# Whole sets of early weight forms, activation tiles in freed form slots, and a last quarter ended in halves: three edits to a decoder-layer kernel on eight cores

## What is computed

```python
u = rms_norm(h, norm_mix_pre)
proj = u @ w_in                      # q, k, v of two attention branches, forget logits, two gates
o_sb, o_fx = stick_breaking(...), forgetting_softmax(...)
merged = sigmoid(g_sb) * (o_sb @ w_branch_sb) + sigmoid(g_fx) * (o_fx @ w_branch_fox)
h = h + rms_norm(merged @ w_out, norm_mix_post)
u2 = rms_norm(h, norm_ffn_pre)
ff = (silu(u2 @ w_gate) * (u2 @ w_up)) @ w_down      # d_ff 5632
return h + rms_norm(ff, norm_ffn_post)
```

## Time and profile before

| what | value |
|---|---|
| median of 3 runs | 3856.3 us (lowest 3856.13) |
| the profiled execution's own time | 3855.46 us |
| its span on the slowest core (core 3), first to last instruction | 3853.9 us |
| spans of the 8 cores | 3804.6 to 3853.9 us |
| PE busy in that span | 94% |

### The profile page before, as it was taken

How to read it: one execution, slowest core, us unless ns; L and a number is a source line. 1 busy time by engine, 2 the same in 40 slices (tenths; PEclk the granted TensorE clock), 3 DMA queues, 4 the chain that set the end, 5 groups by cost and what they waited for, 6 DMA issues and landing times.

```text
span 3853.9 us, 63553 instructions; the slowest of 8 cores (3804.6 to 3853.9 us)
## 1 busy us (share of the span) xinstructions
PE 3633.4 (94%) x21572; PEld 1835.9 (48%) x21572; DVE 1664.3 (43%) x2198; ACT 1468.1 (38%) x2339; POOL 652.5 (17%) x659
## 2 busy tenths in 40 slices
PE   5999899999989989999999899999999999999994
PEld 2566566666644434444444344444444443444442
DVE  3657677677743330122154577444445530000104
ACT  3567687778841112211144343333333321111110
POOL 0000000000011110144204532222222210001322
PEclk9889999999999999999999999999999998999997
DMA  8336654555669887577478975333336657448995
GB/s 217 58 65 101 94 81 80 93 89 88 118 134 212 207 199 204 146 165 172 85 246 264 271 247 187 132 110 110 109 108 203 216 171 198 103 103 209 201 223 179
DMA packets 381774, 597.03 MB, mean 155 GB/s; under 512 B 187792, under 2 KB 240400, under 8 KB 369424
## 3 DMA queue, kind: packets, MB, share of 16 engines
q1 hardware_dynamic: 324832, 391.58, 36.6%
q0 software_dynamic: 35888, 163.63, 23.3%
q10 hardware_dynamic: 20736, 37.76, 2.8%
HBM read 566.66 MB, written 124.78 MB: 179 GB/s over the span
## 4 chain that ended last, share of the span: by engine, by line
PE 73%; DMA 12%; DVE 7%; ACT 3%; issue 3%; POOL 1%; SPq 0%; DVEq 0%; ACTq 0%; POOLq 0%
PE ps L80 73%; DMA fd<-pf 5%; DVE pf L80 2%; DMA mh<-mixs 2%; DMA WT<-W 1%; DVE form L80 1%; ACT pf L80 1%; DMA Ost<-On 1%; DMA hbx<-hs 1%; DVE uT L80 1%; DMA mixs<-mixst 1%; DVE F L80 1%; DMA hb<-hs 1%; ACT L80 0%; ACT sq L80 0%
## 5 line engine op out<-in xcount | busy, mean ns | idle before, releaser
L80 PE MATMUL ps<-F,form 128*128 128x512 bf16 x3584 | 798.9, 381 | 18.1 <-ACT sg L80 18.1
L80 PE MATMUL ps<-as,wd 128*128 128x512 bf16 x2816 | 625.6, 382 | 14.2 <-DMA as<-ad 14.2
L80 PEld LDWEIGHTS ps<-F,form 128*128 128x128 bf16 x3584 | 351.3, 98 | 446.1 <-issue 28.0
L80 PE MATMUL ps<-uT,wbf 128*128 128x512 bf16 x2048 | 500.8, 390 | 22.0 <-DVE uT L80 16.1
L80 PE MATMUL ps<-uT,wgA 128*128 128x512 bf16 x2048 | 456.7, 381 | 0.0
L80 PEld LDWEIGHTS ps<-as,wd 128*128 128x128 bf16 x2816 | 276.1, 98 | 353.3 <-issue 25.5
L80 POOL TENSOR_TENSOR sn<-sn,sn 128x512 f32<-128x512 f32 x176 | 243.4, 1388 | 844.7 <-ACT sn L80 831.8
L80 DVE TENSOR_TENSOR form<-stage 128x1024 bf16<-128x1024 f32 x220 | 298.9, 1379 | 127.0 <-PE ps L80 95.6
L80 PE MATMUL ps<-F,formd 128*128 128x512 bf16 x1344 | 313.5, 381 | 10.8 <-ACT sn L80 6.0
L80 PEld LDWEIGHTS ps<-uT,wbf 128*128 128x128 bf16 x2048 | 200.4, 100 | 246.6 <-issue 69.6
L80 PEld LDWEIGHTS ps<-uT,wgA 128*128 128x128 bf16 x2048 | 201.3, 98 | 243.8 <-issue 5.6
(11 more groups left out here) (111 smaller groups left out, 3374.4 us busy)
## 6 DMA issues: line engine op xcount, KB each, us to landing
stage<-wgu_s SPq DMA_DIRECT2D x44, 2048.0 KB, 9.6
wd<-wfd_t POOLq DMA_DIRECT2D x32, 1408.0 KB, 13.6
formd<-fd SPq DMA_DIRECT2D x168, 256.0 KB, 7.3
wgA<-wg_t POOLq DMA_DIRECT2D x64, 512.0 KB, 8.9
wbf<-wqkv_t POOLq DMA_DIRECT2D x48, 512.0 KB, 7.6
ps<-wgu_s SPq DMA_DIRECT2D x24, 1024.0 KB, 12.3
ad<-ao SPq DMA_DIRECT2D x176, 128.0 KB, 5.4
as<-ad SPq DMA_DIRECT2D x22, 1024.0 KB, 17.9
```

What stands on the lines that cost most here:

```text
L80: ins = getattr(eng, meth)(**kw)
```

## The change

Three edits.

1. `pre_make(j)` makes a whole set: one load of 2 MB into the single tile `ps` (16 KB per partition), seven operations of 128x1024, each into the next of six tiles `pf`, each with a store of its own (256 KB). The load of the next set is issued after the last store of the set. It runs at every second tick (after the second block of a channel tile), so that the 12 sets go out in 24 of the 32 ticks.
2. The `as` tiles 4 to 10 take the seven slots of `F[1]`, one by one, in the order in which the last set's steps are finished with them, and each load is issued right behind that step. Other tiles move to make room.
3. At the end, the held channel tiles do the third quarter (512 tokens), then the last quarter in two halves of 256 tokens. Each half has its own statistics bank, whose sum is added on DVE to that of the 13 earlier channel tiles, its own factor, and its own 16 final items of 256 columns. The gain moves into ACT's eviction copy, so the item's first DVE operation is a plain product; all sums of the end are on DVE, none on POOL. The block banks of this part go round in five, not six.

```diff
-    ps = [at(WO + 20 * i, f"ps{i}", [128, 4, 512], F32, dma=True) for i in range(2)]
-    pf = at(WO + 28, "pf", [128, 7, 512], BF16, dma=True)
+    ps = at(WO + 20, "ps", [128, 4, 1024], F32, dma=True)
+    pf = [at(WO + 2 * i, f"pf{i}", [128, 1024], BF16, dma=True) for i in range(6)]
...
     def pre_make(j):
...
+        for x, p in enumerate(PORD):
+            a_, b_, op = FORM_A[p]
+            dst = pf[(7 * j + x) % 6]
...
+            kb.dma(SP, dst.ds, fd[j, x], dst.t[:, :], reads=[dst.r], writes=[fd_res[j][x]])
+        pre_load(j + 1)
...
-    fl = Filler([pre_make(j) for j in range(2 * N0)], 29)
+    pre_load(0)
+    fl = Filler([(lambda j: (lambda: pre_make(j // 2) if j % 2 == 1 else None))(j) for j in range(2 * N0)], 2 * N0)
     P5(0, fl)
...
+    F1_ORDER = (5, 2, 1, 3, 4, 6, 7)
+    a_off = [22 + 8 * i for i in range(4)] + [108 + 8 * FORM_B[p] for p in F1_ORDER] + [56 + 8 * i for i in range(6)]
...
+        s_, p = steps[n]
+        if j == 0:
+            al.kill(F[1][0].r)
+        if s_ == len(sets) - 1:
+            al.kill(F[1][1][FORM_B[p]])
+            i = 4 + F1_ORDER.index(p)
+            mk_as(i)
+            load_a(0, i)
...
-    for gi in range(4, 11):
-        load_a(0, gi)
...
+                kb.op(DVE, "tensor_tensor", dict(out=ft, in0=ft, in1=rstd3.t[:, col:col + w], op=ALU.mult),
+                      reads=[rstd3.r], writes=[fr])
+                kb.op(DVE if tail else POOL, "tensor_tensor", dict(out=ft, in0=ft, in1=hh_.t[:, 0:w], op=ALU.add),
+                      reads=[hh_.r], writes=[fr])
...
+    f0, i0 = final_items([(c_, 2, 0, 512) for c_ in range(KC)], True)
+    f0()
+    subs = [(0, 0, 512), (1, 0, 256), (1, 256, 256)]
...
+        if w < 512:
+            b2, r2 = banks[6 - lo // 256]
+            kb.op(DVE, "scalar_tensor_tensor", dict(out=rstd2.t[:, 0:w], in0=b2[:, lo:lo + w], scalar=1.0 / D,
+                                                    in1=rstd2.t[:, 0:w], op0=ALU.mult, op1=ALU.add),
+                  writes=[r2, rstd2.r])
...
+    for si, (tc, lo, w) in enumerate(subs):
         for c in range(hold_c, KC):
-            b_ = bank()
-            down_mm(1, wd[(KC + c) % 3], b_[0], b_[1], tc, ALLG, False)
+            b_ = banks[nb["d"] % 5]
+            nb["d"] += 1
+            down_mm(1, wd[(KC + c) % 3], b_[0], b_[1], tc, ALLG, lo, w)
...
+                rstd_part(6 + subs[si - 1][0], subs[si - 1][1], subs[si - 1][2], (512 * (si - 1), 512)[si - 1 > 0])
+                if si == 1:
+                    work += i0
+                else:
+                    f1, i1 = final_items([(c_, 3, 0, 256) for c_ in range(KC)], True)
+                    work += [f1] + i1
+                    step(1)
+            down_ev(1, c, tc, *b_, lo, w)
+            if si > 0:
+                step(5 if si == 1 else 4)
+    step(99)
```

More of the change, by code:

```diff
@@ L1112, in pre_make @@
     def pre_make(j):
[L1113 to L1129, removed]
@@ L1464, in _emit, with stat_w, down_ev @@
     pend = []
-    def down_ev(hf, c, tc, bt, br_):
+    def stat_w(bi, sf, c, lo, w):
+        sb_t, sb_r = banks[bi]
+        first, last = (hold_c if w < 512 else 0), (hold_c - 1 if bi == 7 and hold_c < KC and w == 512 else KC - 1)
+        kb.op(PE, "matmul", dict(out=sb_t[:, lo:lo + w], lhsT=ones_bf, rhs=sf.t[:, 0:w], start=(c == first),
+                                 stop=(c == last)), reads=[sf.r, cbf.r], writes=[sb_r])
+    def down_ev(hf, c, tc, bt, br_, lo=0, w=512):
         fs, sf = ffst[nb["m"] % 2], sqf[nb["m"] % 2]
@@ new lines, in _emit, with step, rstd_part @@
+    f0()
+    subs = [(0, 0, 512), (1, 0, 256), (1, 256, 256)]
+    work = []
+    def step(k):
+        while k > 0 and work:
+            work.pop(0)()
+            k -= 1
+    def rstd_part(bi, lo, w, col):
+        bt, br = banks[bi]
+        kb.op(DVE, "tensor_scalar", dict(out=rstd2.t[:, 0:w], in0=bt[:, lo:lo + w], scalar1=1.0 / D, scalar2=EPS,
+                                         op0=ALU.mult, op1=ALU.add), writes=[br, rstd2.r])
+        if w < 512:
[3 more added lines that the diff above has]
+                  writes=[r2, rstd2.r])
+        kb.op(ACT, "activation", dict(out=rstd2.t[:, 0:w], in_=rstd2.t[:, 0:w], func=AF.Ln), writes=[rstd2.r])
+        kb.op(ACT, "activation", dict(out=rstd3.t[:, col:col + w], in_=rstd2.t[:, 0:w], func=AF.Exp, scale=-0.5),
+              reads=[rstd2.r], writes=[rstd3.r])
@@ new lines, in _emit @@
+                if si == 1:
+                    work += i0
+                else:
+                    f1, i1 = final_items([(c_, 3, 0, 256) for c_ in range(KC)], True)
[5 more added lines that the diff above has]
+    step(99)
+    while pend:
+        stat_w(*pend.pop(0))
+    rstd_part(7, 256, 256, 768)
+    f1, i1 = final_items([(c_, 3, 256, 256) for c_ in range(KC)], True)
@@ L1556, in _emit @@
+    f1()
+    work += i1
+    step(99)
     finish()
```

146 lines of the change are left out of this document (63 added, 83 removed).

## The result

The changed kernel takes 3832.0 us (median of 5 runs; 3882.9 us for the kernel before, whose 5 runs include the three that gave 3856.3). The ratio of the two is 0.989, 95% interval 0.985 to 0.993: faster, by about 1%, and by less than the 2% of which the prediction spoke. The ratios here leave out runs in which a die showed a lower clock; the medians contain them. The forecast was 3805.5, a ratio of 0.987, with a range of 3789 to 3838. So the time lies in the range, 26.5 us above the forecast. The change is smaller than it looks from there: 50 us less were forecast, and against the 3856.3 us from which the prediction started 24 came. Why, the parts of the sum show.

What follows compares the result with a forecast made beforehand. PE was taken to bound the kernel, with 94% of the span. From the profiled 3855.5 us, less 35.2 (merge stage) and 21.3 (down start), plus 6.5 (end), came 3805.5 us; range 3789 to 3838.

Steps and rivals of the forecast that it cites:

- I take 21.2: Merge stage: DMA time per set and channel tile in us, 0.5 short of PE's pace; gain 35.2 us.
- the play of 9.5 us: Merge stage: a set may start up to 9.5 us late before PE waits for the next block's products.
- the sets fall behind: Merge stage rival: 23.2 us per set, gain 16, kernel 3825; sets behind or loads late together got chance 0.22.
- the full figure: Merge stage: at 358 GB/s a channel tile's 7.1 MB take 19.8 us, sets just keep pace, gain 39.2 us.
- most of them start before the end, so the last lands at about 3167 to 3173: Down start: early loads of `as4` to `as10`, 20 us for 7.3 MB, leave 0.5 us lost; gain 21.3 us.
- +1.4: Start of the end part: first block reuses the preceding block's bank and waits 1.4 us for its two evictions.
- 2 x (0.426 + 0.11) = 1.07: End: us per half item of 256 columns, two DVE operations with gaps; 16 items take 17.1 us.
- the span ends 8.0 us later: End: in the kernel before, the span ends 8.0 us after the 16 last items finish at 3845.9.
- 0.87 us an item: End: half's item at the skill table's 58 fixed cycles, end 6 us earlier, about even; set aside for 1.07.
- a second factor: End: the second half's factor, queued behind all 16 first-half items on DVE, is not hidden and costs 2.1 us.

Runs made afterwards that it cites:

- the six profiles: Profiles of the changed kernel and five experimental kernels with the same merge stage; over all 48 cores that stage has a median of 322.4 us.
- slower pace: Changed kernel with its 12 sets spread over 30 of the 32 ticks, not 24: merge stage 312.3 us against 327.8, kernel ratio 0.988.
- fewer bytes: Changed kernel without loading branch weights of channel tiles 2 to 15 in the first half's merge stage (output not the layer's): merge stage 312.0 us.
- the quarters: Changed kernel with the load tile cut into four, each quadrant reloaded after the last form that reads it, forms reordered: merge stage 325.4 us.
- everything else together: Changed kernel plus 30-tick pace, `wd2` and `as11` to `as16` behind `as10`, banks one later, next product first: end 69.4 us whole blocks, 69.5 halves.
- the POOL experiment: Changed kernel with every other sum of the last quarter's items on POOL: end 75.2 us against 71.4, tail 9.0 us on every core.

## Why the prediction was right and wrong

**The errors of the sum cancel in part, which is luck.** Against the table: 18 us too much for the merge stage (5 of them because core 3 had more to lose than the median core), 10 too much for the down start, 12 too little for the end, 17 too much in all; the middle was right. What failed is the period of a set in the merge stage, a load left out of the down start, and two carried-over times at the end.

**Merge stage: "I take 21.2".** The mechanism was right: making 9.7 us, the products queued behind the seventh form, the play of 9.5 us. The mis-sized term, and the step that failed, is the period: 22.4 to 22.7 us, because the load was costed at the pace that it has alone. The weights cost what they did: 43.3% of 260 us for 18.78 MB, 36 loads, is 3.14 us each, 9.4 us for three. That leaves 11.8 us of the 21.2 for load and stores of a set, 5.6 of it the load at its lone pace; queue 1 spent 54.4% of 260 us on 44.16 MB, 3.2 us per MB, which is 12.6 us for the set's 3.94 MB. With engines at 98% that makes 22.5. So a set misses PE's pace by 1.8 us, not 0.5, and over eleven periods by 19 to 20, twice the slack. The rival "the sets fall behind" named this with 16 us of gain left; 17.1 was measured, 22 over the six profiles. The slower pace and the fewer bytes show the cause from two sides, the quarters exclude the chain.

The Trainium skill ("DMA: Bandwidth & Descriptors", section Bandwidth) says that the HBM side, some 358 GB/s for a core, is what binds such transfers. The profile counts the weights as they land, in bf16 (512 KB for a tile of 128x2048); in HBM they are float32 and twice as large. So from 1140 to 1400 us the core moved 44.16 MB and, at HBM, twice 18.78 MB: 314 GB/s, 88% of that figure, with the DMA engines 98% busy. At the full figure the sets would have kept pace, as the prediction worked out, and they did not; whether HBM or the engines set the 314, no run here shows.

**Down start: "most of them start before the end, so the last lands at about 3167 to 3173".** The seven loads were costed as if alone. The step that failed is a term put at nothing: the weight `wd2`, which POOL's queue issues as soon as its place is free (3159.23) and which took a third of the engines for 25 us, though PE wants it only after the second channel tile. The queues of the slowest core, 3160 to 3185 us:

```profile
q1 hardware_dynamic: 2514, 4.68, 63.2%
q0 software_dynamic: 144, 1.44, 35.6%
```

With the weight kept behind `as10`, the gain is 19.6 us (62.4 to 42.8), near the 21.3 predicted. The lower clock behind PE's wait made the loss 2.7 us larger than the 6.5 us waited.

**Middle: "+1.4".** Right where it stands. Whether it lengthens the kernel isn't shown, as the end hangs on DVE: from the first down matmul to the end, the kernel with both loads held back and without this wait took 666.8 us, the one with the weight held back and with this wait 667.2.

**End: "2 x (0.426 + 0.11) = 1.07", and "the span ends 8.0 us later".** Both were carried over from rows that don't fit. The 0.11 us behind an operation is there only where the next one reads its result; an operation that doesn't starts some 0.08 us before the last one ends. An item is 0.52 + 0.345, and 32 items are 6.6 us cheaper than said. (The 0.87 us an item that the prediction set aside came out as a number only: one operation does take 0.42 us, and it was the gaps that were wrong.) The 8.0 us tail belonged to POOL, which the change takes out: 5.8 us. The rest held: the third quarter's first item comes 4.7 us sooner after its block and the last 4.2, and a second factor lies on the path (2.3 us, 2.1 said). Without the halves the change would have been some 4 us faster still, though with everything else together halves and whole blocks end alike. What paid most in part 3 was taking the sums from POOL: half of the last quarter's sums put back cost 3.8 of the 6.9 us.

## What to carry to other kernels

Where a side job feeds on the same DMA queues as the main one, cost it by the queues' busy share in that very stage, not by a lone transfer, and give it all the ticks there are: one number, the pace, was worth 10 to 15 us here, beside 17 to 22 for the rebuilding. When loads are brought forward, look at what else becomes free to issue at that moment on other queues and hold back what is needed late. Price a chain of operations by their start-to-start times in the order in which they will stand, and look at the end of the span for time in which nothing runs.

## What was not expected of the hardware

- DVE operations that don't depend on each other overlap: 0.335 us from start to start at 0.42 us each (256 columns, float32), 0.60 at 0.69 (512 columns).
- With POOL at work until near the end, the span ends 4 to 7 us after the last transfer, with everything idle (kernel before and the POOL experiment, all cores); in the changed kernel it ends about 1 us after.
- How long the attention stage takes differs from core to core and run to run by up to 60 us, and with it which core is the slowest. The stretch 0 to 1077 us of the run after, core 6 first, then core 3 (columns as above; the clock is the third number from the end):

```profile
0.00:1077.00 1077.00, 981.26 (x9246) 646.60 (x9383) 707.63 (x1069) 762.09 (x1201) 41.02 (x83) 0.94 0.59 97
...
0.00:1077.00 1077.00, 998.28 (x9624) 652.06 (x9625) 735.34 (x1112) 794.76 (x1255) 42.45 (x85) 0.98 0.58 102
```

  Core 6 had a mean granted clock of 0.94 and core 3 of 0.98, under the same program. Why was not looked into.
